# A fused two-block transformer kernel: the opening worked by blocks of tokens, and the final norm's squares taken inside the last projections

## The reference

```python
h = concat([meta_tokens, x])                       # 16 meta tokens, then x[512, 1024]
u = rmsnorm(h, norm_mix_w)                         # h / sqrt(mean(h^2) + eps) * w
proj = u @ w_in                                    # -> linear attention + sliding-window attention
h = h + concat([o_gla, o_swa]) @ w_out
h = h + square(relu(rmsnorm(h, norm_ff_w) @ w_ff1)) @ w_ff2
x = rmsnorm(h, final_norm_w)[16:]                  # end of the first block

mods = silu(c) @ w_ada + b_ada                     # nine vectors: shifts, scales, gates
x = x + 0.5*gt1 * swiglu(modulated rmsnorm(x))     # hidden width 2816
x = x + gt2 * (merge of differential attention and an mLSTM branch) @ w_out
x = x + 0.5*gt3 * swiglu(modulated rmsnorm(x))     # the last projections
return rmsnorm(x, g_final)                         # the final norm
```

## Time and profile before

| | |
|---|---|
| median of 3 runs | 2049.88 us (2049.44 to 2054.54) |
| the profiled execution | 2053.37 us |
| its span, first to last instruction | 2051.3 us |
| PE busy | 1985.4 us, 97% |
| DVE, ACT, POOL busy | 56%, 38%, 18% |
| mean granted clock of PE | 0.987 |
| DMA share in the first, second and third fortieth (51.3 us each) | 6, 3, 2 tenths |

### The profile page before, as it was taken

The page is one execution under the profiler, slowest core; times in us unless marked ns, Lnnn a source line. Parts: engine busy times, 40 slices in busy tenths (PEclk is TensorE's granted clock), DMA queues, the critical chain, the costliest instruction groups (busy, mean ns, idle before and its releaser), DMA issues.

```text
span 2051.3 us, 25776 instructions
## 1 busy us (share of the span) xinstructions
PE 1985.4 (97%) x9676; PEld 1591.6 (78%) x9676; DVE 1142.3 (56%) x1742; ACT 778.6 (38%) x1323; POOL 371.1 (18%) x307
## 2 busy tenths in 40 slices
PE   7999999999999999999999999999999999999996
PEld 6876688888888788888888877777666788888885
DVE  6576667667667665453554366564534754444453
ACT  6436332223325222222332355657556342222222
POOL 3000029999200694000000000000000000000000
PEclk9999999999999999999999999999999999999998
DMA  6321136666332664333254433323215423323321
GB/s 157 89 63 31 43 123 207 203 204 204 123 92 62 176 202 134 102 91 94 82 143 129 114 112 107 106 93 129 72 57 190 123 72 103 97 87 102 98 86 51
DMA packets 275166, 233.59 MB, mean 114 GB/s; under 512 B 16707, under 2 KB 248510, under 8 KB 274544
## 3 DMA queue, kind: packets, MB, share of 16 engines
q1 hardware_dynamic: 255216, 164.19, 27.5%
q0 software_dynamic: 18256, 62.92, 9.7%
q10 hardware_dynamic: 1616, 5.44, 1.1%
HBM read 215.41 MB, written 12.58 MB: 111 GB/s over the span
## 4 chain that ended last, share of the span: by engine, by line
PE 89%; DVE 6%; ACT 3%; issue 1%; DMA 1%; ACTq 0%; POOL 0%; SPq 0%; DVEq 0%
PE bank L1103 26%; PE bank L1105 26%; PE bank L1104 26%; PE bank L1586 1%; PE bank L1704 1%; PE bank L1569 1%; DVE wlo L1790 1%; PE bank L1722 1%; PE bank L1272 1%; PE bank L1418 1%; PE bank L1699 1%; PE bank L1320 1%; PE bank L1157 1%; ACT whi L546 0%; PE bank L1170 0%
## 5 line engine op out<-in xcount | busy, mean ns | idle before, releaser
L1103 PE MATMUL bank<-xhi,whi 128*128 128x512 f32 x1768 | 702.3, 397 | 11.0 <-DVE xlo L1796 5.0
L1105 PE MATMUL bank<-xhi,wlo 128*128 128x512 f32 x1768 | 691.6, 391 | 0.0
L1104 PE MATMUL bank<-xlo,whi 128*128 128x512 f32 x1768 | 690.6, 391 | 0.0
L1790 DVE TENSOR_TENSOR wlo<-stage,whi 128x1024 fp32r<-128x1024 f32 x309 | 409.1, 1335 | 208.8 <-ACT whi L546 208.3
L546 ACT ACTIVATE whi<-stage 128x1024 fp32r<-128x1024 f32 x309 | 321.2, 1051 | 414.6 <-PE bank L1105 381.6
L1103 PEld LDWEIGHTS bank<-xhi,whi 128*128 128x128 f32 x1768 | 333.1, 188 | 89.5 <-issue 14.7
L1105 PEld LDWEIGHTS bank<-xhi,wlo 128*128 128x128 f32 x1768 | 332.8, 188 | 71.3
L1104 PEld LDWEIGHTS bank<-xlo,whi 128*128 128x128 f32 x1768 | 333.4, 189 | 66.4
L2130 DVE SCALAR_TENSOR_TENSOR H<-bank,sc,H 128x512 f32<-128x512 f32 x304 | 219.6, 748 | 84.0 <-PE bank L1105 83.5
L1103 PE MATMUL bank<-hidhi,whi 128*128 128x512 f32 x608 | 241.9, 398 | 3.1 <-DVE hidlo L2155 3.0
L1105 PE MATMUL bank<-hidhi,wlo 128*128 128x512 f32 x608 | 238.5, 392 | 0.0
(11 more groups left out here) (408 smaller groups left out, 1816.5 us busy)
## 6 DMA issues: line engine op xcount, KB each, us to landing
arena<-in_w_ada POOLq DMA_DIRECT2D x72, 512.0 KB, 3.9
stage<-in_w_in SPq DMA_DIRECT2D x71, 512.0 KB, 3.9
stage<-in_w_ff SPq DMA_DIRECT2D x64, 512.0 KB, 4.3
stage<-in_w_gate SPq DMA_DIRECT2D x44, 512.0 KB, 4.7
stage<-in_w_up SPq DMA_DIRECT2D x44, 512.0 KB, 3.9
stage<-in_w_down SPq DMA_DIRECT2D x44, 512.0 KB, 3.8
arena<-arena ACTq DMA_DIRECT2D x16, 256.0 KB, 5.4
stage<-in_w_proj_a SPq DMA_DIRECT2D x8, 512.0 KB, 4.0
```

Of the source, the lines that this page charges most:

```text
L1103: mm(out, sh, mh, start=start, stop=False, **kw)
L1104: mm(out, sh, ml, start=False, stop=False, **kw)
L1105: return mm(out, sl, mh, start=False, stop=stop, **kw)
L1790: V.tensor_tensor(wlo[:, static % SPLITS, :], stage[:, static % STAGES, :], whi[:, static % SPLITS, :].bitcast(F32), ALU.subtract).then_in ...
```

## The change

It has two parts.

**Opening by blocks of tokens.** SP loads the meta tokens ahead of `x`. ACT also loads `norm_mix_w` by itself (8 rows). ACT takes the square root block by block, and DVE makes the normalised rows of a block as soon as its root is there. PE turns half a block of raw rows into one bank (`turn_half`, four transposes), three such halves ahead of the projection and five (`turn_rest`) after it. The copies into `H` are by half block: DVE five, ACT three, three of the eight ahead of the second projection's split. The transposes of the parameters move into the first projection. The small steps `wsq`, `lam` and `silu_c` move into a function `parameters`, behind the first projection.

**The end.** ACT squares each tile of `H` as it is added and also scales it by the final norm's weight (`weighted`), DVE sums the squares between its adds, PE sums over partitions by four products with one column. PE turns the weighted tiles. The eight outputs are only scaled by the row's factor, four on ACT and four on DVE, and SP stores them.

Eight semaphores that count to one are joined into one, `act_once`, in the order in which ACT signals them.

```diff
+            sp.dma_start(mrow, t["meta_tokens"]).then_inc(s("meta_loaded"), 16)
             for b in range(NB):
                 sp.dma_start(xrow[b], t["x"][0, b * P:(b + 1) * P, :]).then_inc(s(f"x_loaded{b}"), 16)
-            sp.dma_start(mrow, t["meta_tokens"]).then_inc(s("meta_loaded"), 16)
 
             def load(c):
...
+            for i in range(2 * NB):
+                half, b = divmod(i, NB)
+                sp.wait_ge(s("y_odd") if i % 2 else s("y_even"), i // 2 + 1)
+                sp.dma_start(out[0, b * P:(b + 1) * P, half * T:(half + 1) * T], tl(i)).then_inc(s("y_stored"), 16)
+            sp.wait_ge(s("y_stored"), 16 * 2 * NB)
...
+            act.dma_start(first_w, t["norm_mix_w"].rearrange("a (r p) -> (a r) p", p=P)).then_inc(s("ident_loaded"), 16)
             act.wait_ge(s("consts"), 1)
             A_(small[:, 255:256], eps[:, 0:1], ACT.Sqrt)
+            act.wait_ge(s("meta_loaded"), 16)
+            link(A_(mnorm, mrow, ACT.Square, accum_out=ss5[0:META, NB:NB + 1]))
+            A_(std5[:, NB:NB + 1], ss5[:, NB:NB + 1], ACT.Sqrt, scale=1.0 / D, bias=eps[:, 0:1]).then_inc(s("std_ready"), 1)
             for b in range(NB):
                 act.wait_ge(s(f"x_loaded{b}"), 16)
...
+                link(A_(xnorm[b], xrow[b], ACT.Square, accum_out=ss5[:, b:b + 1]))
+                A_(std5[:, b:b + 1], ss5[:, b:b + 1], ACT.Sqrt, scale=1.0 / D, bias=eps[:, 0:1]).then_inc(s("x_std"), 1)
...
-                if kt in (1, 3):
-                    hi(1 + kt // 2)
...
+            hi(1)
+            copy_half(2)
+            hi(2)
...
+                if c == 0:
+                    for i in (6, 7):
+                        copy_half(i)
+                    parameters()
                 if c in (3, 7):
                     meta_sum(c // 3 + 1)
...
-            for i in range(2 * NB):
+            for kt in range(KT):
+                if kt == 2:
+                    A_(small[:, 255:256], eps[:, 1:2], ACT.Sqrt)
+                square(6, kt)
+                A_(weighted[kt], H[:, kt, :], ACT.Copy, scale=pc("g_final_2", kt)).then_inc(s("y_weighted"), 1)
+            act.wait_ge(s("sq_used"), STD_NO[6] - 1)
+            A_(yss[:, 0:4], bank[3][:, 0:NB], ACT.Sqrt, scale=1.0 / D, bias=eps[:, 1:2]).then_inc(s("std_ready"), 1)
+            act.wait_ge(s("y_rstd"), 1)
+            for i in range(0, 2 * NB, 2):
                 act.wait_ge(s("y_t"), i + 1)
-                ins = A_(tl(16 + i), bank[ybank(i)][:, :], ACT.Square, accum_out=yss[:, i:i + 1])
...
+                    ins = nc.tensor.transpose(bank[half_bank[i]][:, q * P:(q + 1) * P],
+                                              xrow[b][:, (4 * half + q) * P:(4 * half + q + 1) * P], ident[:, :])
+                ins.then_inc(s("x_turned"), 1)
...
+            ins.then_inc(s("meta_turned"), 1)
+            for i in range(3):
+                turn_half(i)
+            for b in range(NB):
+                pe.wait_ge(s("xn_made"), b + 2)
+                for kt in range(4):
+                    ins = turn_rows(kt, b)
+                    if b == NB - 1:
+                        ins.then_inc(s("xt_done"), 1)
+                if b == NB - 2:
+                    idle_products(6, 0)
...
-                        turn_rows(kt + 4)
+                        for b in range(NB):
+                            ins = turn_rows(kt + 4, b)
+                        ins.then_inc(s("xt_done"), 1)
+                    if kt == 5:
+                        pe.wait_ge(s("um_ready"), 1)
+                        pe.wait_ge(s("par_loaded"), 16 * len(PARAMS))
+                        nc.tensor.transpose(bank[3][:, 288:412], tl(10)[0:124, 0:P], ident[0:124, 0:124])
+                        nc.tensor.transpose(bank[3][:, 412:484], tl(11)[0:72, 0:P], ident[0:72, 0:72]).then_inc(s("meta_turned"), 1)
...
+            def turn_rest():
+
+                for i in range(3, 2 * NB):
+                    if i == 7:
+                        pe.wait_ge(s("start_copied"), 1)
+                    turn_half(i)
...
+                pe.wait_ge(s("x_copied"), 2 * NB - len(BY_ACT))
+                pe.wait_ge(s("start_copied"), len(BY_ACT))
...
+                    turn_rest()
                 if c in (1, 3, 7):
...
+            pe.wait_ge(H_added, norm_H[6] + KT)
+            for q in range(3):
+                pe.wait_ge(s("y_weighted"), 5 + q)
+                for i in range(NB, 2 * NB - 1):
+                    y_turn(i, q)
+            pe.wait_ge(s("sq_summed"), 5 * SUM_NO[6] + KT - 1)
+            for b in range(NB):
+                ins = mm(bank[3][:, b:b + 1], sq_sum[:, b * P:(b + 1) * P], ones[:, 0:1], start=(b == 0), stop=True, skip_group_check=True)
+            ins.then_inc(s("sq_used"), 1)
+            pe.wait_ge(s("y_weighted"), KT)
+            for i in range(NB, 2 * NB - 1):
+                y_turn(i, 3).then_inc(s("y_t"), 1)
+            pe.wait_ge(s("std_ready"), STD_NO[6])
+            for q in range(4):
+                ins = y_turn(2 * NB - 1, q)
+            ins.then_inc(s("y_t"), 1)
...
+            def normal_rows(b):
+
+                dve.wait_ge(s("x_std"), b + 1)
+                link(V.reciprocal(rstd5[:, b:b + 1], std5[:, b:b + 1]))
+                V.tensor_scalar(xnorm[b], xrow[b], rstd5[:, b:b + 1], None, ALU.mult).then_inc(s("xn_made"), 1)
+
...
+            normal_rows(0)
+            dve.wait_ge(s("meta_turned"), 2)
+            V.tensor_tensor(um[:, :, 0:META], bank[3][:, 0:P].rearrange("p (k t) -> p k t", k=KT),
+                            g.unsqueeze(2).to_broadcast([P, KT, META]), ALU.mult).then_inc(s("um_ready"), 1)
+            copy_half(0)
+            normal_rows(1)
+            copy_half(1)
+            normal_rows(2)
+            normal_rows(3)
...
+                if kt == 6:
+                    dve.wait_ge(s("meta_turned"), 3)
+                    link(V.tensor_copy(par[:, KT:196], bank[3][:, 288 + KT:484]))
...
+            lo(1)
+            for i in range(3, 2 * NB):
+                if i not in BY_ACT:
+                    copy_half(i)
+            lo(2)
...
-            dve.wait_ge(s("yss_ready"), 1)
-            link(V.tensor_tensor(yss[:, 0:4], yss[:, 0:4], yss[:, 4:8], ALU.add))
-            V.tensor_copy(yss[:, 8:9], yss[:, 0:1]).then_inc(s("ysum"), 1)
-            dve.wait_ge(s("ystd"), 1)
-            link(V.reciprocal(yss[:, 4:8], yss[:, 0:4]))
-            dve.wait_ge(s("grow_in"), 16)
-            for n in range(2 * NB):
-                b, half = divmod(n, 2)
-                V.scalar_tensor_tensor(out=tl(n), in0=bank[ybank(NB * half + b)][:, :], scalar=yss[:, 4 + b:5 + b],
-                                       in1=grow[:, half * T:(half + 1) * T], op0=ALU.mult, op1=ALU.mult).then_inc(s("y_out"), 1)
+                ffn_group(g, C_FFB, 6, lambda x: gate_half[:, 8 + x:9 + x], lambda j: (C_FFB + 6 * g + j + AHEAD,),
+                          6 if g == G_FF2 - 1 else None)
+
+            for kt in range(KT - 2, KT):
+                sum_square(6, kt)
+            dve.wait_ge(s("std_ready"), STD_NO[6])
+            V.reciprocal(yss[:, 4:8], yss[:, 0:4]).then_inc(s("y_rstd"), 1)
+            dve.wait_ge(s("y_rstd"), 1)
+            for i in range(1, 2 * NB, 2):
+                dve.wait_ge(s("y_t"), i + 1)
+                V.tensor_scalar(tl(i), bank[ybank(i)][:, :], yss[:, 4 + i % NB:5 + i % NB], None, ALU.mult).then_inc(s("y_odd"), 1)
...
-            for n in range(2 * NB):
-                pool.wait_ge(s("y_out"), n + 1)
-                pool.dma_start(out[0, (n // 2) * P:(n // 2 + 1) * P, (n % 2) * T:(n % 2 + 1) * T], tl(n)).then_inc(s("y_stored"), 16)
-            pool.wait_ge(s("y_stored"), 16 * 2 * NB)
 
 
```

More of the change, by code:

```diff
@@ L423, in build @@
         obuf = [tabs[:, :, 0:T], gg[:, :, 0:T]]
-        grow, yss = tl(8, 2), small[:, 0:16]
+        weighted, yss = [tl(16 + k) for k in range(KT)], small[:, 0:16]
         ybank = lambda i: (i + 4) % 8
@@ L605, in _, with copy_half @@
-            act.wait_ge(s("um_ready"), 1)
-            A_(wsq, wsq, ACT.Sqrt, bias=eps[:, 1:2])
-            act.wait_ge(s("lam_sums"), 1)
-            A_(lam[:, 2:4], lam[:, 0:2], ACT.Exp).then_inc(s("lam_exp"), 1)
-            A_(silu_c, par[:, pcol["c_2"]:pcol["c_2"] + KT], ACT.Silu).then_inc(s("silu_c"), 1)
+            def copy_half(i):
+                b, half = divmod(i, 2)
+                act.wait_ge(s("x_turned"), i + 1)
+                A_(H[:, 4 * half:4 * half + 4, b * P:(b + 1) * P], bank[half_bank[i]][:, :].rearrange("p (q t) -> p q t", q=4),
+                   ACT.Copy).then_inc(s("start_copied"), 1)
@@ L611, in level_decay, with parameters @@
+            hi(1)
+            copy_half(2)
+            hi(2)
+            def parameters():
+                act.wait_ge(s("um_ready"), 2)
+                A_(wsq, wsq, ACT.Sqrt, bias=eps[:, 1:2])
+                act.wait_ge(s("lam_sums"), 1)
+                A_(lam[:, 2:4], lam[:, 0:2], ACT.Exp).then_inc(s("act_once"), 1)
```

(15 more changed lines are left out.)

119 lines of the change are left out of this document (50 added, 69 removed).

## The result

| | before | after |
|---|---|---|
| median | 2049.88 us (5 runs) | 2038.34 us (5 runs, 2031.60 to 2042.31) |
| ratio after to before | | 0.9942, 95% interval 0.9930 to 0.9955 |
| the profiled execution | 2053.37 us | 2031.60 us |
| its span, mean granted clock | 2051.3 us, 0.987 | 2029.6 us, 0.994 |
| start of the first product of a projection | 21.86 us | 15.17 us |

The change makes the kernel 11.5 us faster by the medians, 0.58%. The direction with most of my chance (no difference that can be told) was wrong too.

A forecast was written before the change was run, and what follows sets the result against it. PE, busy for 97% of the span, bounds the kernel, so gains lie before and behind its stream: 3.5 (opening) + 1.2 (end) = 4.7 us, a span of 2046.6 and a median of 2045.2 us, range 2042.0 to 2048.7.

The forecast's parts named there:

- no difference that can be told: Whole kernel: a measured time between 2043.7 and 2056.0 us, within about 0.3% of no change; chance 0.67.
- The end: From the last group's adds to the last store: gives 1.2 us, with 0 to 2.5 allowed for stores by SP.
- the term for the engine of the stores: At the end, SP issues right behind the first output, without POOL's 0.28 us between 2037.66 and 2037.94.
- Rival 2: Both ends give more: no clock fall behind the 16-row products (1.7), or shorter store tail (up to 1.3); 2042.2 to 2043.6; 0.24.
- The other part of the end: Squares in the stream and outputs on two engines: outputs begin at 2035.9 instead of 2036.90, 1.0 us earlier.
- My own sign of a wrong end: The end is wrong if the adds of `H` end more than 2 us later than PE's products.
- The opening: From loading `x` to the second projection, which starts at 26.3 instead of 29.76: gives 3.5 us.
- the start: First transposes of the first projection begin at 15.7 instead of 21.50, 5.8 us earlier.
- the unread products: Six PE products at 0.25 us behind the third block's rows, until 13.8, set the first projection's start.
- Rival 1: PE's clock, low in the opening or falling at the meta products, takes 1.7 or 3.4 us; 2046.9 to 2048.6; chance 0.24.
- rival 3: PE stays at the lower clock through the first projection, costing 11.0 us: slower, 2056.2; chance 0.05.
- Rival 4: At the end, squares in the stream bring nothing, ACT or SP's stores being later: 3.5 remains, 2046.4; chance 0.07.

The follow-up runs named there:

- experiments 1 and 2: 1: the changed kernel with its stores back on POOL, median 2042.92 us; 2: the kernel before with its stores on SP, median 2044.36 us.
- experiment 8: The changed kernel with two unread products in the opening in place of six; median 2037.67 us.

## Why the prediction was wrong

**The end, the step that failed.** I wrote that the end gives 1.2 us, and of the stores by SP: "From above I allow 2.5, should part of the empty 6 us at the end be POOL's". What failed is the term for the engine of the stores. It stood in the sum with some 0.3, the issue alone, and in the range with at most 1.3 more; experiments 1 and 2 measured 5.9 and 6.3 us. Of that, 4.9 and 5.1 lie behind the last landing, where the drain is, and 1.0 and 1.2 are stores that land sooner. I had seen the empty 6 us in the earlier trace rows and said that nothing explains them. The view by source line of the exit, 148, has the row of a DRAIN of 4.88 us on POOL in the profile of the kernel before. The bound of 2.5 came from no row at all, and the landing time of a load by SP, which I named beside it, is only the reason for the bound from below. Rival 2 named the right place ("the tail behind the last store shrinks with SP in POOL's place") with a price of 1.3, a fifth of the true one.

The other part of the end came out as forecast, outputs 1.0 earlier by the sum and 1.1 measured, and 1.1 to 1.6 for the squares with the outputs on two engines by experiments 1 and 2. But the path was not the one that I gave, so the hit is in part luck. I had ACT as the slowest engine, with eight pairs and the load one behind another. ACT does hold the chain until the load is over. From the sum of the third tile on it is DVE, whose sums stand between its adds: 1.26 us for each tile, where ACT's pair takes 1.13 to 1.16. I had no price for these sums, except for the last. My own sign of a wrong end is there too: the last add of `H` ends at 2018.6, 2.9 us behind PE's last product (2015.7), and I had set the limit at 2.

**The opening.** Forecast 3.5, measured 4.5 at the second projection, 4.7 at product 160 with the fall of the clock at its new place, and 6.1 there in a profile without. The mechanism held in each part: 7.9 us forecast from the first transposes to the meta products' start, 7.8 measured; 2.3 forecast for `turn_rest`, 2.33 measured. The term that was off is the start, 14.78 where I had 15.7. I had put the meta tokens' square in one queue with the blocks' from 5.0 on. It ran at 3.23, ahead of them, so the last root was done at 11.0 and not 12.0. The third block's rows were turned by 11.62 and not 12.3, and the unread products took 1.34, not 1.5. What I missed is the weight split, which ends within 0.1 us of the path that I gave (experiment 8).

**Rival 1 and rival 3, the clock.** The clock rose earlier, not later. Line 1203's twelve transposes took 421 ns or more, and those of line 1208 fell to 272 behind 10.0, where before the change the last of line 1180 at 421 ns begins at 13.87. PE starts on the blocks of `x` 2.6 us earlier, at 6.74. Transposes of the kernel after, line 1208 in the stretch from 12 to 14 us:

```profile
L1208 PE MATMUL bank<-ident,arena x4: 272/272/273, 12.8 to 13.1; 128*128 128x128 f32 x4
```

The rule of the Trainium skill ("TensorE: Matmul & The Clock Gate", Part 4: PE-mode transpose), that the full clock doesn't engage for transposes, is again not what the trace shows: only transposes ran before the fall from 421 to 272. No fall came at `turn_rest`. The other half of rival 2, the fall that doesn't come, is true in half of the profiles.

**Rival 4** is false: the outputs come 1.1 us earlier, and SP's stores land sooner, not later.

**The sum.** With the engine of the stores at 6.1 (the mean of 5.9 and 6.3) in place of 0.3 the same working gives 10.6 (3.5, 1.0 and 6.1), and with the opening's measured 4.7 it gives 11.8. The medians say 11.5. The chance of 0.67 for "no difference that can be told" came from an empty stretch left unexplained, in which the change exchanged the very engine.

## What to carry to other kernels

Where a program's span ends with microseconds in which no engine works, look for what each engine does at its exit before bounding it. In every profile here GpSimd's exit takes over 4 us, so its last instruction, even a bare wait, should lie well ahead of the end, and the last stores belong to an engine with a short exit. Put a table load where its engine stands idle, and count whose queue a helpful extra product joins: the bound may already be there.

## What the runs showed of the hardware that was not expected

- Stores by SP land sooner than the same stores by POOL: 2.2 us in the median against 2.9 with the outputs of before, 2.9 against 3.3 with those of the changed kernel. In each half microsecond between the first and the last data the DMA engines moved 254 to 393 GB/s before and 373 to 397 after.
- The point at which PE's 128x128 transposes fall from 421 to 272 ns moved between 9.8 and 11.9 us from profile to profile, with PE's instructions the same until the first of these times.
- In the stream the lower level of the clock comes for 3.4 to 10.2 us at a time, mostly at the same places of the program (near 190, 205, 275, 640, 1020, 1400, 1655 us), but not at each place in each run. The times of one kernel go with it and spread over 8 to 11 us.
